# Float32r projections with the weights stationary: 256 tokens streamed, evacuated in transposed order, without staged transposes

## The reference, cut to what matters

```python
def attn_mixer(xn, ...):
    proj = xn @ w_in                       # 2048 -> 5656 columns
    q_a, kv_a, g_a, q_b, k_b, v_b = jnp.split(proj, [o1, o2, o3, o4, o5], axis=-1)
    kv_a = kv_a.reshape(b, s, 6, NSA_KV, NSA_HD)
    kc = compress(kv_a[:, :, 0], pe_k, w1_k, w2_k)
    vc = compress(kv_a[:, :, 1], pe_v, w1_v, w2_v)
    ...

def rglru_mixer(xn, w_in, conv_w, conv_b, wa, ba, wx, bx, lam_p, w_out):
    xb, yb = jnp.split(xn @ w_in, 2, axis=-1)
    y = jax.nn.gelu(yb)
    xc = <causal depthwise convolution of width 4 over the tokens of xb> + conv_b
    ...                                    # gates r, i from xc; scan over the tokens
    return (h.astype(xn.dtype) * y) @ w_out
```

## Time and profile before

| | |
|---|---|
| median of 3 runs | 2381.69 us (2381.62 to 2382.73) |
| profiled execution | 2381.88 us |
| its span | 2380.2 us |
| PE busy | 2355.1 us, 99% |
| PEld busy | 1950.3 us, 82% |
| DVE busy | 1565.5 us, 66% |
| ACT busy | 1140.6 us, 48% |
| HBM read | 440 MB, mean 186 GB/s |

### The profile page before, as it was taken

How to read it: one execution, slowest core, us unless ns; L and a number is a source line. 1 busy time by engine, 2 the same in 40 slices (tenths; PEclk the granted TensorE clock), 3 DMA queues, 4 the chain that set the end, 5 groups by cost and what they waited for, 6 DMA issues and landing times.

```text
span 2380.2 us, 29364 instructions
## 1 busy us (share of the span) xinstructions
PE 2355.1 (99%) x10770; PEld 1950.3 (82%) x10770; DVE 1565.5 (66%) x2208; ACT 1140.6 (48%) x1478; POOL 8.5 (0%) x31
## 2 busy tenths in 40 slices
PE   9999999999999999999999999999999999999998
PEld 7888778888888888888888888888888888888886
DVE  5555678676676676666596777866676676666655
ACT  5435564544444444444554575554444444444454
POOL 0000000000000000000000000000000000000000
PEclk9999999999999999999999999999999999999999
DMA  7744436666666665665568455566666666555564
GB/s 223 246 127 122 143 126 201 188 194 194 193 187 196 193 192 194 194 194 195 179 199 259 128 158 182 188 195 194 194 187 197 191 191 195 193 194 194 194 206 140
DMA packets 234331, 443.85 MB, mean 186 GB/s; under 512 B 16217, under 2 KB 21377, under 8 KB 234113
## 3 DMA queue, kind: packets, MB, share of 16 engines
q1 hardware_dynamic: 234192, 442.62, 58.8%
q10 hardware_dynamic: 48, 0.02, 0.0%
HBM read 440.49 MB, written 2.10 MB: 186 GB/s over the span
## 4 chain that ended last, share of the span: by engine, by line
PE 91%; DVE 3%; ACT 3%; issue 1%; DMA 1%; SPq 0%; ACTq 0%; DVEq 0%
PE ps L1440 29%; PE ps L1442 29%; PE ps L1441 29%; ACT w_hi L617 1%; PE ps L1656 1%; DVE w_lo L884 1%; PE ps L1392 1%; ACT prob L799 1%; DVE prob L1210 1%; DMA raw<-in_w_in_rec_dram 1%; SPq L526 0%; PE ps L1568 0%; DMA lam_in<-in_diff_lk_dram 0%; DVE o_all L1249 0%; ACT junk L684 0%
## 5 line engine op out<-in xcount | busy, mean ns | idle before, releaser
L884 DVE TENSOR_TENSOR w_lo<-raw,w_hi 128x1024 fp32r<-128x1024 f32 x820 | 998.5, 1220 | 737.2 <-ACT w_hi L617 731.1
L617 ACT ACTIVATE w_hi<-raw 128x1024 fp32r<-128x1024 f32 x820 | 862.8, 1055 | 1023.2 <-PE ps L1442 994.1
L1440 PE MATMUL ps<-w_hi,xa_hi 128*128 128x512 f32 x1664 | 647.7, 389 | 0.0
L1442 PE MATMUL ps<-w_hi,xa_lo 128*128 128x512 f32 x1664 | 647.4, 389 | 0.0
L1441 PE MATMUL ps<-w_lo,xa_hi 128*128 128x512 f32 x1664 | 647.3, 389 | 0.0
L1440 PEld LDWEIGHTS ps<-w_hi,xa_hi 128*128 128x128 f32 x1664 | 312.4, 188 | 64.7
L1441 PEld LDWEIGHTS ps<-w_lo,xa_hi 128*128 128x128 f32 x1664 | 312.4, 188 | 64.7
L1442 PEld LDWEIGHTS ps<-w_hi,xa_lo 128*128 128x128 f32 x1664 | 312.4, 188 | 64.7
L1440 PE MATMUL ps<-w_hi,xb_hi 128*128 128x512 f32 x864 | 350.3, 405 | 3.9 <-DVE xb_lo L953 2.3
L1442 PE MATMUL ps<-w_hi,xb_lo 128*128 128x512 f32 x864 | 337.6, 391 | 0.0
L1441 PE MATMUL ps<-w_lo,xb_hi 128*128 128x512 f32 x864 | 337.1, 390 | 0.0
(11 more groups left out here) (230 smaller groups left out, 1014.7 us busy)
## 6 DMA issues: line engine op xcount, KB each, us to landing
raw<-in_w_ffn_gate_dram SPq DMA_DIRECT2D x176, 512.0 KB, 3.5
raw<-in_w_ffn_up_dram SPq DMA_DIRECT2D x176, 512.0 KB, 3.6
raw<-in_w_ffn_down_dram SPq DMA_DIRECT2D x176, 512.0 KB, 4.5
raw<-in_w_in_attn_dram SPq DMA_DIRECT2D x88, 512.0 KB, 3.5
raw<-in_w_ple_gate_dram SPq DMA_DIRECT2D x64, 512.0 KB, 4.7
raw<-in_w_in_rec_dram SPq DMA_DIRECT2D x64, 512.0 KB, 4.3
raw<-in_w_out_attn_dram SPq DMA_DIRECT2D x32, 512.0 KB, 3.8
raw<-in_w_out_rec_dram SPq DMA_DIRECT2D x32, 512.0 KB, 4.3
```

What stands on the lines that cost most here:

```text
L617: nc.scalar.activation(w_hi[:, s, 0:n], raw[:, s, 0:n], ACT.Copy).then_inc(hi_ready, 1)
L884: nc.vector.tensor_tensor(w_lo[:, s, 0:n], raw[:, s, 0:n], w_hi[:, s, 0:n].bitcast(F32), ALU.subtract).then_inc(lo_ready, 1)
L1440: nc.tensor.matmul(o, xh[:, k, tok], w_hi[:, s, wk], start=(k == 0), stop=False)
L1442: ins = nc.tensor.matmul(o, xl[:, k, tok], w_hi[:, s, wk], start=False, stop=(k == nkt - 1))
```

## The change

Fifteen chunks (qa 2, kvc, qk0 2, qk1 2, and in layer 1 xb 4 and yb 4), and kvs and kvw, get an attribute `across`. For them `across_slot` makes the 128x128 weight block the stationary operand and streams the 256 tokens, so the result lands in PSUM already transposed: 2 k-tiles x 4 blocks x 3 = 24 matmuls of 256 columns per slot. In kvs and kvw the two key blocks are done so; for the values the activation tile stays stationary and 256 value columns stream, also 24 matmuls. `turn`, the copies of `aftermath` and the staging go. Because 1/rms now varies along the free axis, a row of it is needed on every partition: `spread_rstd` (DVE) and `turn_rstd` (PE, two transposes) make it once per layer, and the first evacuation copies it to `rrow`. `evacuate_across` on DVE, at j = 3, multiplies the two banks (1024 elements) by that row straight into the destination; for the keys of qk0 and qk1 four products of 64 partitions into the `kz` pairs. For yb it writes to `stage`'s space, and ACT applies the gelu from there to `yT` (`gelu_rows`), also at j = 3. The waits on `turn_used` become waits on these evacuations, and the last group of AT_PROD and AT_SPLIT moves from 67 to 65.

```diff
--- before.py
+++ after.py
@@ -96,19 +97,19 @@
         ph.append(Phase(name, 1, slots, kinds, "B", cols, ("w_in_attn", "w_in_attn"),
                         first_turn=first, norm=0))
 
-    qk = Kind("qk", "a", 2)
+    qk = Kind("qk", "v", across=4)
     vb = Kind("vb", "v")
     attn("qa", (qk, qk), (Q_A, Q_A + CW), first=True)
-    attn("gkvc", (Kind("gates", "v", 2), Kind("kvc", "v", 2)), (G_A, KV_A), slots=(4, 8))
-    attn("kvsw", (Kind("kvs", "v", 1), Kind("kvw", "v", 1)), (KV_A + CW, KV_A + 2 * CW))
+    attn("gkvc", (Kind("gates", "v", 2), Kind("kvc", "v", across=4)), (G_A, KV_A), slots=(4, 8))
+    attn("kvsw", (Kind("kvs", "v", across=2), Kind("kvw", "v", across=2)), (KV_A + CW, KV_A + 2 * CW))
     attn("qk0", (qk, qk), (Q_B, K_B))
     attn("qk1", (qk, qk), (Q_B + CW, K_B + CW))
     attn("vb", (vb, vb), (V_B, V_B + CW))
     for layer in range(2):
         if layer:
-            ph.append(Phase("xb", 2, (8, 8), (Kind("xb", "v", 2),) * 2, "B", (0, CW),
+            ph.append(Phase("xb", 2, (8, 8), (Kind("xb", "v", across=4),) * 2, "B", (0, CW),
                             ("w_in_rec",) * 2, first_turn=True, norm=3))
-            ph.append(Phase("yb", 2, (8, 8), (Kind("yb", "a", 2),) * 2, "B", (D, D + CW),
+            ph.append(Phase("yb", 2, (8, 8), (Kind("yb", "v", across=4),) * 2, "B", (D, D + CW),
                             ("w_in_rec",) * 2, norm=3))
         ph.append(Phase(f"out{layer}", 2, (8, 8), (resid, resid), "B", (0, CW),
@@ -250,8 +251,8 @@
-AT_PROD = {44: 0, 52: 1, 60: 2, 67: 3}
-AT_SPLIT = {59: 0, 61: 1, 63: 2, 67: 3}
+AT_PROD = {44: 0, 52: 1, 60: 2, 65: 3}
+AT_SPLIT = {59: 0, 61: 1, 63: 2, 65: 3}
 
@@ -360,6 +361,10 @@
+        row_of = {0: 0, 3: 1}
+        rb = [at("rb_a", [NT, P], F32, s_off + 13312), at("rb_r", [NT, P], F32, s_off + 54528)]
+        rrow = [at("rrow_a", [S], F32, s_off + 12288), at("rrow_r", [S], F32, s_off + 53504)]
+
@@ -639,12 +648,13 @@
-                    else:
-                        if m == 0:
-                            act.wait_ge(turned, turn_no(q, i, r))
-                        ins = nc.scalar.activation(stage[:, m], acc, ACT.Copy if kind == "qk" else
-                                                   ACT.Gelu_apprx_tanh, scale=rs)
                 ins.then_inc(sg_ready if kind == "ple" else evac["a"], 1)
+
+            def gelu_rows(i, r):
+
+                c = 2 * i + r
+                act.wait_ge(evac["v"], evac_no(named["yb"], i, r)[1])
+                nc.scalar.activation(yT[:, 4 * c:4 * c + 4], across_stage, ACT.Gelu_apprx_tanh).then_inc(y_ready, 1)
 
@@ -728,6 +738,8 @@
                         evacuate(*prev)
+                    if j == 3 and prev[0].name == "yb":
+                        gelu_rows(*prev[1:])
@@ -884,6 +896,43 @@
+            def spread_rstd(stat):
+
+                for m in range(NT):
+                    ins = nc.vector.tensor_scalar(rb[row_of[stat]][:, m], ident[:], 0.0, rstd[:, stat, m:m + 1],
+                                                  ALU.mult, ALU.add)
+                ins.then_inc(rb_made, 1)
+
+            def evacuate_across(q, i, r):
+
+                name, n, c = q.name, row_of[q.norm], 4 * (2 * i + r)
+                if name in ("qa", "xb") and (i, r) == (0, 0):
+                    dve.wait_ge(rb_turned, n + 1)
+                    nc.vector.tensor_copy(rrow[n][:], ps[:, EX, 0:S]).then_inc(rrow_ready, 1)
+                dve.wait_ge(rrow_ready, n + 1)
+                if name == "yb" and c:
+                    dve.wait_ge(y_ready, c // 4)
+                if name in ("qk0", "qk1") and r == 1:
+                    for b in range(2):
+                        for z, rows in enumerate((slice(0, DQK), slice(DQK, P))):
+                            ins = nc.vector.tensor_tensor(
+                                kz_pair(4 * (name == "qk1") + 2 * b)[rows, :, z, :],
+                                ps[rows, 2 * r + b, :].rearrange("p (f t) -> p f t", f=2),
+                                rrow[n][rows].unsqueeze(1).to_broadcast([DQK, 2, S]), ALU.mult)
+                    ins.then_inc(evac["v"], 1)
+                    return
+                nf = q.kinds[r].across
+                if name == "kvsw":
+                    for m in range(NT):
+                        nc.vector.tensor_scalar(vtok[:, r, m], ps[:, 2 * r + 1, m * S:(m + 1) * S],
+                                                rstd[:, q.norm, m:m + 1], None, ALU.mult)
+                o = {"qa": lambda: qaT[:, c:c + 4], "qk0": lambda: qbT[:, 0:4], "qk1": lambda: qbT[:, 4:8],
+                     "gkvc": lambda: cmpT[:], "kvsw": lambda: kT[:, r],
+                     "xb": lambda: xbT[:, c:c + 4, 3:3 + S], "yb": lambda: across_stage}[name]()
+                src = ps[:, 2 * r:2 * r + nf // 2, :].rearrange("p b (f t) -> p (b f) t", f=2)
+                nc.vector.tensor_tensor(o, src, rrow[n][:].unsqueeze(1).to_broadcast([P, nf, S]), ALU.mult
+                                        ).then_inc(evac["v"], 1)
+
             def evacuate(q, i, r):
                 k = q.kinds[r]
                 kind = k.name
...
@@ -1002,32 +1047,18 @@
-                        if k.name == "gates":
-                            nc.vector.tensor_scalar(gates_sb[:, b], ps[:, TP + (t0 + b) % 2, 0:NGATE],
-                                                    rstd[:, 0, b:b + 1], None, ALU.mult).then_inc(turn_used, 1)
-                            continue
-                        src = ps[:, TP + (t0 + b) % 2, :].rearrange("p (f t) -> p f t", f=2)
-                        c = 4 * r + 2 * b
-                        g = 4 * (q.name == "qk1") + 2 * b
-                        if k.name == "qk" and q.name != "qa" and r == 1:
-                            for z, rows in enumerate((slice(0, DQK), slice(DQK, P))):
-                                ins = nc.vector.tensor_copy(kz_pair(g)[rows, :, z, :], src[rows])
-                            ins.then_inc(turn_used, 1)
-                            continue
-                        o = {"qa": lambda: qaT[:, c:c + 2],
-                             "qk0": lambda: qbT[:, g:g + 2], "qk1": lambda: qbT[:, g:g + 2],
-                             "gkvc": lambda: cmpT[:, 2 * b:2 * b + 2], "kvsw": lambda: kT[:, r],
-                             "xb": lambda: xbT[:, 8 * i + c:8 * i + c + 2, 3:3 + S],
-                             "yb": lambda: yT[:, 8 * i + c:8 * i + c + 2]}[q.name]()
-                        nc.vector.tensor_copy(o, src).then_inc(turn_used, 1)
+                        nc.vector.tensor_scalar(gates_sb[:, b], ps[:, TP + (t0 + b) % 2, 0:NGATE],
+                                                rstd[:, 0, b:b + 1], None, ALU.mult).then_inc(turn_used, 1)
+                if q.stat == 3 and col == 3:
+                    spread_rstd(3)
-                dve.wait_ge(turn_used, named["xb"].turn0 + 2 * c + 2)
+                dve.wait_ge(evac["v"], evac_no(named["xb"], *divmod(c, 2))[1])
@@ -1063,6 +1094,7 @@
                     if q.name == "qa" and j == 2:
                         mean_square(0)
+                        spread_rstd(0)
@@ -1341,7 +1373,7 @@
-                    dve.wait_ge(turn_used, named["yb"].turn0 + 2 * (g + 1))
+                    dve.wait_ge(y_ready, g + 1)
...
@@ -1444,6 +1479,35 @@
+            def across_slot(q, r, j):
+                s, (k0, nk, _, w) = ring_place(None, j), slot_shape(q, r, j)
+                (xh, xl), nf = X[q.src], q.kinds[r].across
+                for k in range(k0, k0 + nk):
+                    w0 = (k - k0) * w
+                    for f in range(nf):
+                        o = ps[:, 2 * r + f // 2, (f % 2) * S:(f % 2 + 1) * S]
+                        wf = slice(w0 + f * P, w0 + (f + 1) * P)
+                        nc.tensor.matmul(o, w_hi[:, s, wf], xh[:, k], start=(k == 0 and f % 2 == 0), stop=False)
+                        nc.tensor.matmul(o, w_lo[:, s, wf], xh[:, k], start=False, stop=False)
+                        ins = nc.tensor.matmul(o, w_hi[:, s, wf], xl[:, k], start=False,
+                                               stop=(k == KD - 1 and f % 2 == 1))
+                    for m in range(NT if nf == 2 else 0):
+                        o = ps[:, 2 * r + 1, m * S:(m + 1) * S]
+                        tok, wv = slice(m * P, (m + 1) * P), slice(w0 + S, w0 + 2 * S)
+                        nc.tensor.matmul(o, xh[:, k, tok], w_hi[:, s, wv], start=(k == 0 and m == 0), stop=False)
+                        nc.tensor.matmul(o, xh[:, k, tok], w_lo[:, s, wv], start=False, stop=False)
+                        ins = nc.tensor.matmul(o, xl[:, k, tok], w_hi[:, s, wv], start=False,
+                                               stop=(k == KD - 1 and m == NT - 1))
+                ins.then_inc(w_used, 1)
+            def turn_rstd(n):
+                pe.wait_ge(rb_made, n + 1)
+                for m in range(NT):
+                    ins = nc.tensor.transpose(ps[:, EX, m * P:(m + 1) * P], rb[n][:, m], ident[:])
+                ins.then_inc(rb_turned, 1)
@@ -1463,13 +1527,15 @@
```

(31 more changed lines are left out.)

## The result

The changed kernel took **2391.86 us** (median of 6 runs, 2389.77 to 2393.59), the kernel before 2381.37 on the same chip (6 runs, 2379.86 to 2382.73): a ratio of 1.0043, 95% interval 1.0033 to 1.0053. It is 0.4% slower; forecast was 2378.1, in a range from 2368 to 2390. The profiled execution of the changed kernel took 2393.59 us, 11.7 more than that of before.

The account below looks back on a forecast made before the run. PE's stream plus its waits was taken to bound the kernel. Terms 1.0 - 5.24 - 6.2 + 1.7 + 6.35 - 1.24 = -3.6; 2381.88 - 3.6 - 0.19 gave 2378.1 us, range 2368 to 2390.

Parts of the forecast that it names:

- Part 1: Matmuls in 136 converted slots: 256 columns start 114.0 ns apart; +2.1 us, about half covered by PE's waits, so +1.0.
- the load is a fixed cost: Rival, 20%: converted slots run at 120 ns and lose 22 us, less 2 for DMA waits and 3 in yb: 2394.
- decisive point, a pace of 116: Pace of 256-column matmuls above which the fixed-load rival outweighs the other terms' 4.6 us, if half is covered; otherwise 114.8.
- The 4.3 us that the prediction works out from it: Extra cost of the 136 converted slots by the skill's formula, 215.8 ns for 512 columns and 109.2 for 256.
- Part 2, the turns: Removed transposes of `stage`, 0.885 us per turn of 8 on PE: -5.24 us in layer 0, -6.2 in layer 1.
- qa's two and xb's first: Turns said to bring nothing, lost in PE's weight waits at ring slot 28 and behind the lru weights.
- Part 3: Added rstd transposes on PE, VectorE operations and copy: 0, covered by later waits and early `w_lo`; uncovered VectorE work 1 us per layer.
- Part 4: Evacuation moved to DVE at j = 3: keys +1.7 us, yb +6.35, out1's wait -1.24.
- The keys' lump: qk0 and qk1: 2.81 us of DVE products before attention's coefficient holds PE 1.15 us, twice: 2.3; net +1.7.
- the copies that went: Where the key evacuation of qk0 and qk1 stood before, PE waited too; its removal gives back say 0.6 us.
- The yb chain: yb: ACT's gelu waits for DVE's product and delays the next w_hi; PE stalls at slots 44 and 53 to 60, +6.35 us.
- The end of out1's wait: Last group of AT_PROD and AT_SPLIT moves two slots ahead, so out1's wait at 1479.56 goes: -1.24 us.

Follow-up runs that it names:

- pace alone: Kernel before, staging and transposes kept, with the 136 slots' 512-column streams cut into halves of 256 columns: 2395.17 us, ratio 1.0057.
- experiment 5: Changed kernel with `turn_rstd` after slot 8 instead of 9: 2390.18 us; kernel before with both 1/rms rows made, turned, copied but unused: 2381.47 us.
- experiment 2: Kernel before with the 136 slots' 512-column streams cut into halves of 256, same operands, order and turns: 2395.17 us, ratio 1.0057.
- experiments 4 and 3: Changed kernel with yb's gelu at j = 4: 2387.73 us; changed kernel with key products spread over j = 3 to 6: 2386.35 us.

## Why the prediction was wrong

**Part 1 failed: the pace, 120.0 ns measured for 114.0.** I had both bounds, 113.3 and 120, and took 114.0, "nearest to the gates", since the gates' distance was exactly half of that of 512 columns and "the excess seems to go with the columns, not with the load". Behind a full load the excess is the same 13.4 ns for 512 and for 256 columns. The exact half was a coincidence of two different loads: 213.3 + 13.4 behind 128 columns, and 106.7 + 6.6 behind 24. The forecast +1.0 is +15.5 in the profiled phases (14.1 in the runs); the rival "the load is a fixed cost" gave 2394 with 20%, against 2391.86. Its decisive point, a pace of 116, is passed, so its mechanism is borne out; that its number came so near is in part luck, since it had the pace 4.5 too large and the turns 2.8 too small a gain, against keys, queries and row too cheap by 2.9, 1.6 and 4.2. The earlier trace rows spoke neither for nor against it: 128 streamed columns run at the 111 ns floor of a full load in both cases. What would have decided was the form of the neighbour: the gates row differs from the new matmul in the loaded columns, the 512-column row only in the streamed ones, and it is the latter's excess that should have been carried over.

The Trainium skill's formula of the page "TensorE: Matmul & The Clock Gate", section "Back-to-back issue gap", N/2.4 + 2.5 ns, which the page gives for the isolated matmul, has the form that these runs show, a fixed term per matmul, but the term in this stream of loads and matmuls is 13.4 ns and not 2.5. (The 4.3 us that the prediction works out from it are 4.1 without rounding.) The Trainium skill's other sentence in that section, that load and matmul together set the spacing in a real stream (81 ns at 128 columns, 131 at 512), holds in kind and not in its figures: 128 columns take 111 ns behind a full load and 60 behind one of 24 columns, and 512 take 226.7.

**Part 2, the turns: right in price, wrong in which come back.** Each slot with a removed turn takes 0.64 us less (3.52 to 2.88), which is 0.80 less 0.16 of pace, and the restart of 0.09 in the next slot goes too: 0.885. Slot by slot against "pace alone" all seventeen turns came back, 14.2 us; the forecast had 11.4, since it gave up qa's two and xb's first. For qa it was wrong: ring slot 28 was not bound by its weights any more (its `w_lo` 1.9 us early, behind a slower PE). xb's first came back in slots 11 and 12 too, but PE then waits at slot 16, as forecast, so that much of what slots 15 to 17 lose (part 3) is this turn again.

**Part 3, "0", is not right in the profile.** The cover that I named, early `w_lo`, held for PE's next slots. But the transposes themselves cost PE 0.2 us per layer, and I counted DVE's work and left out its wait for them (3.67 us). SP, which refills a slot when `w_lo` is made, stands behind it: the transfer for slot 16 went out 1.8 us later, with and without the new pace. Whether PE loses by that is not shown, since in most traces this transfer lands right behind the lru weights in any case (experiment 5), which is the wait that the forecast had named. The size stays open between 0 and 2 us in the runs; the changed kernel's profiled execution has 0.4 for the transposes and 3.7 in slots 15 to 17, 4.2 in all.

**Part 4.** The keys' lump was in the right place and too small. I let it hold PE by its length less the slack, once for each chunk, 2.3 in all; in fact PE waited 2.86 us, and the following weight slot was late too (ring slots 77 and 78: +2.7 and +1.6 over "pace alone", and slot 61 +1.6: 5.8), of which spreading gives back 4.3. Slots 45 and 66 to 68 are 1.2 us shorter than with the pace alone; I put that down to the copies that went (forecast 0.6), and no run tests it. The forecast had no term at all for the queries' product, which stands before attention's operations as well: PE waits 0.50 us for `o_all` in ring slot 54, and slots 53, 54 and 62 are 1.6 longer than with the pace alone. The yb chain was right in mechanism and too large: 2.5 for 6.35, and before slots 57 and 60, with nothing at 44. The rival for the pace had a reason, "a slower PE runs less into the yb chain", which no run tests by itself. The end of out1's wait was right: slot 69 went from 3.96 to 2.72 us, -1.24 (-1.4 with the next slot, against "pace alone").

Put together: 15.5 for the pace, -14.2 for the turns, +5.8 for the keys, -1.2 for the copies, +1.6 for the queries, +2.5 for yb, +4.2 for the row and slots 15 to 17, -1.4 for out1: +12.8 in the profiled phases. The profiled executions as wholes differ by 11.7, the medians by 10.5.

## What to carry to other kernels

When an operation is cut into shorter ones, carry over the excess per instruction of the row that shares the larger part of its form (here the loaded columns), and take the fixed cost as the likely case until a row excludes it: that two distances stand at an exact half is no evidence. An instruction that moves to a single engine should be traced to the next waiter in its queue, wait and work both. A form that costs a little per slot and saves a fixed piece (here 1.28 against 0.885 us per chunk) pays only where PE stands still anyway, so convert chunk by chunk and start with the chunk whose result is waited for last.

## What the runs showed of the hardware

- A float32r matmul behind a full 128-column load starts N/2.4 + 13.4 ns after the one before (N of 256, 384, 512), and about 111 ns with N of 128 and 192; behind 24 or 64 columns 256 take 113.5, behind 96 116. Which operand is loaded, weights or activations, makes no difference (120 ns for 256 columns in the changed kernel and in experiment 2).
- Behind only 24 or 64 loaded columns, 512 streamed ones take more than behind 128: 232 and 230 ns for 226.7. I have no reason for it.
- The issue of one and the same DMA of 2 MB on SP lasted 0.47, 1.30 or 1.50 us, and that of the 512 KB weight transfer after it 4.3, 6.0 and 5.4 us, in three executions of the same code of xb (experiments 4 and 3, the changed kernel); PE's loss in slots 15 to 17 was 0, 1.6 and 3.7 us.
- A 512 KB transfer issued on SP behind two of 2 MB landed 1.3 to 1.5 us after the second of them in ten of eleven executions, though its own issue began anywhere from 29.2 to 33.0 us after xb's start, 10 us and more before that.
